# Squares of the residual stream summed by halves, a root chain with one step less, and a wait of GpSimd on its own last piece

## The reference

```python
xf * lax.rsqrt(jnp.mean(xf * xf, axis=-1, keepdims=True) + EPS) * g
```

## Time and profile before

| | us |
|---|---|
| median of three runs (lowest, highest) | 1600.02 (1599.84, 1602.06) |
| the profiled execution | 1606.23 |
| its span, first to last instruction | 1604.4 |
| PE busy (share of the span) | 1527.9 (95%) |
| POOL busy | 1224.2 (76%) |
| ACT busy | 714.9 (45%) |
| DVE busy | 689.3 (43%) |
| mean granted PE clock, as a share of full speed | 0.983 |

### The profile page before, as it was taken

The page is one execution under the profiler, slowest core; times in us unless marked ns, Lnnn a source line. Parts: engine busy times, 40 slices in busy tenths (PEclk is TensorE's granted clock), DMA queues, the critical chain, the costliest instruction groups (busy, mean ns, idle before and its releaser), DMA issues.

```text
span 1604.4 us, 21660 instructions
## 1 busy us (share of the span) xinstructions
PE 1527.9 (95%) x7010; PEld 1165.5 (73%) x7010; DVE 689.3 (43%) x1306; ACT 714.9 (45%) x881; POOL 1224.2 (76%) x1184
## 2 busy tenths in 40 slices
PE   7999999999999999989999999999999899999986
PEld 5777877788887778877788887888785656646535
DVE  3996854311116986834310037265544122122115
ACT  4554453544446544534544455546341422415323
POOL 6998898888899996888888898977591733639623
PEclk9999999999999999999999999998999999999997
DMA  6754454677765553455677655645364998999990
GB/s 210 224 168 135 132 157 134 190 227 214 228 203 162 166 158 117 132 145 152 192 231 217 189 173 172 203 132 171 91 208 152 343 337 341 346 390 396 397 358 28
DMA packets 95958, 333.84 MB, mean 208 GB/s; under 512 B 11184, under 2 KB 15808, under 8 KB 94944
## 3 DMA queue, kind: packets, MB, share of 16 engines
q1 hardware_dynamic: 88240, 307.26, 58.2%
q10 hardware_dynamic: 6480, 21.22, 4.3%
q0 software_dynamic: 1152, 4.19, 0.7%
HBM read 322.12 MB, written 21.00 MB: 214 GB/s over the span
## 4 chain that ended last, share of the span: by engine, by line
POOL 44%; PE 32%; issue 18%; DMA 2%; DVE 2%; ACT 1%; POOLq 1%; ACTq 0%; DVEq 0%; SPq 0%
POOL w_lo L1897 43%; PE bank L691 7%; PE bank L1206 5%; PE bank L695 4%; PE bank L1274 3%; PE bank L1224 3%; PE bank L1243 3%; PE bank L1297 2%; PE bank L1337 1%; DMA arena<-in_experts 1%; DMA logits<-outputs_by_expert,tiny 1%; ACT w_hi L1450 1%; POOL w_lo L1912 1%; PE bank L1106 1%; PE bank L730 1%
## 5 line engine op out<-in xcount | busy, mean ns | idle before, releaser
L1897 POOL TENSOR_TENSOR w_lo<-raw,w_hi 128x256 fp32r<-128x256 f32 (+1 forms) x1092 | 1030.8, 978 | 165.6 <-ACT w_hi L1450 163.1
L1450 ACT ACTIVATE w_hi<-raw 128x1024 fp32r<-128x1024 f32 x371 | 392.8, 1059 | 529.1 <-PE bank L695 283.0
L691 PE MATMUL bank<-w_hi,hT 128*128 128x512 f32 x2240 | 601.4, 401 | 25.4 <-DVE hT L2013 5.9
L691 PEld LDWEIGHTS bank<-w_hi,hT 128*128 128x128 f32 x2240 | 420.8, 192 | 123.0 <-issue 11.8
L695 PE MATMUL bank<-w_lo,hT 128*128 128x512 f32 x1120 | 329.9, 396 | 6.6 <-POOL w_lo L1897 6.5
L695 PEld LDWEIGHTS bank<-w_lo,hT 128*128 128x128 f32 x1120 | 212.5, 191 | 57.5 <-POOL w_lo L1897 12.0
L1912 POOL TENSOR_TENSOR w_lo<-arena,w_hi 128x1024 fp32r<-128x1024 f32 x61 | 144.4, 2388 | 126.5 <-ACT w_hi L1450 126.3
L2316 DVE SCALAR_TENSOR_TENSOR arena<-bank,tiny,arena 128x256 f32<-128x256 f32 x44 | 21.1, 484 | 170.7 <-ACT arena L1611 153.6
L1450 ACT ACTIVATE w_hi<-arena 128x1024 fp32r<-128x1024 f32 x61 | 64.0, 1057 | 57.8 <-PE bank L1206 28.7
L1006 PE MATMUL bank<-w_hi,mixT 128*128 128x512 f32 x352 | 88.0, 390 | 0.0
L691 PE MATMUL bank<-w_hi,mixT 128*128 128x512 f32 x288 | 78.7, 397 | 2.5 <-DVE xn L2290 2.5
(11 more groups left out here) (390 smaller groups left out, 1883.5 us busy)
## 6 DMA issues: line engine op xcount, KB each, us to landing
raw<-in_stream SPq DMA_DIRECT2D x357, 512.0 KB, 3.6
arena<-in_experts SPq DMA_DIRECT2D x154, 512.0 KB, 11.3
raw<-in_experts SPq DMA_DIRECT2D x38, 512.0 KB, 9.5
rows_by_expert<-in_blank ACTq DMA_DIRECT2D x56, 128.0 KB, 3.9
arena<-in_stream SPq DMA_DIRECT2D x9, 512.0 KB, 14.3
gates<-rows_by_expert SPq DMA_DIRECT2D x3, 1024.0 KB, 7.3
outputs_by_expert<-xn ACTq DMA_DIRECT2D x3, 1024.0 KB, 8.4
bias_skewed<-bias_windows SPq DMA_DIRECT2D x4, 512.0 KB, 5.0
```

What stands on the lines that cost most here:

```text
L691: pe.matmul(LIN[t][:, :], lhs[:, a, k0 + k, t * P:(t + 1) * P], w, start=(k0 + k == 0 and a == 0), stop=False)
L1450: act.activation(w_hi[:, s, :], src, ACT.Copy).then_inc(s_hi, 1)
L1897: part = nc.gpsimd.tensor_tensor(w_lo[:, i, c], raw[:, i, c], w_hi[:, i, c].bitcast(F32), ALU.subtract)
```

## The change

- `rounds`: where a quarter is made in more than one piece, GpSimd now waits, after each quarter, until its own last piece has raised s_lo.
- `root_inverse` and `refined`: t = -0.5 t v in one operation, and the result (t + 1.5) r in one. The operation that made -0.5 t + 1.5 by itself is gone. The order of the multiplications is another, the value the same up to rounding.
- `x_stats` calls `both_halves`: the squares of the second half (two of 128 x 512, into columns 2 and 3) and a sum of two columns each. The first half's squares now stand at four places ahead of it: before the first splits of the program; in `x_back`, after the adds of half 0 and a wait on them, ahead of the adds of half 1; and in `layer`, after residual(0), ahead of the second norm's first splits.
- `second` likewise; the subtraction for sw moves behind the first pair of splits, and the squares' scrap output goes to xn in place of xs.

```diff
--- before.py
+++ after.py
@@ -1897,6 +1897,8 @@
                             part = nc.gpsimd.tensor_tensor(w_lo[:, i, c], raw[:, i, c], w_hi[:, i, c].bitcast(F32),
                                                            ALU.subtract)
                         part.then_inc(s_lo, 1)
+                        if parts > 1:
+                            pool.wait_ge(s_lo, r * RING + (i + 1))
 
             per_layer, ff = LAYER_Q // RING, 6 * (FF_GROUPS - 1) // RING
             for l in range(LAYERS):
@@ -1972,10 +1974,13 @@
                 if meanwhile:
                     meanwhile()
                 root_inverse(n)
-                last = dve.tensor_tensor(tiny[:, to:to + n], r, t, ALU.mult)
+                last = refined(tiny[:, to:to + n], r, t)
                 if to == 32:
                     own(last)
                 return last
+
+            def refined(out, r, t):
+                return dve.scalar_tensor_tensor(out, t, 1.5, r, ALU.add, ALU.mult)
 
             def root_inverse(n):
 
@@ -1983,17 +1988,21 @@
                 dve.wait_ge(s_std, std.up())
                 own(dve.reciprocal(r, s))
                 own(dve.tensor_tensor(t, r, r, ALU.mult))
-                own(dve.tensor_tensor(t, t, v, ALU.mult))
-                own(dve.tensor_scalar(t, t, -0.5, 1.5, ALU.mult, ALU.add))
-
-            def x_squares():
+                own(dve.scalar_tensor_tensor(t, t, -0.5, v, ALU.mult, ALU.mult))
+
+            def half_squares(n):
                 for t in range(TT):
-                    i = squares(x[:, t, :], xn[:, t, :], D, t)
+                    cols = slice(n * 512, (n + 1) * 512)
+                    i = squares(x[:, t, cols], xn[:, t, cols], D, 2 * n + t)
                 own(i)
 
+            def both_halves():
+                half_squares(1)
+                own(dve.tensor_tensor(tiny[:, 0:2], tiny[:, 0:2], tiny[:, 2:4], ALU.add))
+
             def x_stats(gain):
 
-                x_squares()
+                both_halves()
                 split(hT, KT // 2, gain, KT // 2)
                 rstd(2, X_INV).then_inc(s_rs, 1)
                 dve.wait_ge(s_rs, rs.up())
@@ -2335,7 +2344,9 @@
                     dve.wait_ge(s_used, pos.up())
                     v = x[:, 1, n * 512:(n + 1) * 512]
                     dve.tensor_tensor(v, AB[2 + n][:, :], v, ALU.add).then_inc(s_x, 1)
-                dve.wait_ge(s_x, xr.up(2))
+                    dve.wait_ge(s_x, xr.up())
+                    if n == 0:
+                        half_squares(0)
 
             def next_gain():
                 dve.wait_ge(s_sm, smc.up(32))
@@ -2491,12 +2503,6 @@
             def rows_normed(t):
                 dve.wait_ge(s_grow, 16)
                 dve.scalar_tensor_tensor(normed_rows[:, t, :], x[:, t, :], tc(X_INV, t), gain_row, ALU.mult, ALU.mult).then_inc(s_norm, 1)
-
-            def half_squares(n):
-                for t in range(TT):
-                    cols = slice(n * 512, (n + 1) * 512)
-                    i = squares(x[:, t, cols], xn[:, t, cols], D, 2 * n + t)
-                own(i)
 
             def place():
 
@@ -2669,11 +2675,10 @@
                 dve.wait_ge(s_x, xr.up(2))
 
             def second():
+                both_halves()
+                split(hT, QK, S_N1, KT // 2)
                 dve.wait_ge(s_sw, 1)
                 dve.tensor_tensor(sw[:, 1, :], small[:, S_SW:S_END], sw[:, 0, :].bitcast(F32), ALU.subtract).then_inc(s_nx, 1)
-                for t in range(TT):
-                    squares(x[:, t, :], xs[:, t, :], D, t)
-                split(hT, QK, S_N1, KT // 2)
                 for t in range(TT):
                     i = dve.tensor_tensor(xn[:, t, :], x[:, t, :], gain1, ALU.mult)
                 own(i)
@@ -2686,8 +2691,8 @@
                 own(dve.tensor_scalar(mean_x, mean_x, EPS, None, ALU.add))
                 dve.scalar_tensor_tensor(mean_xn, mean_x, EPS, mean_xn, ALU.mult, ALU.add).then_inc(s_var, 1)
                 root_inverse(4)
-                dve.tensor_tensor(tiny[:, X_INV:X_INV + 2], tiny[:, 34:36], tiny[:, 50:52], ALU.mult).then_inc(s_rs, 1)
-                own(dve.tensor_tensor(first_inv, tiny[:, 32:34], tiny[:, 48:50], ALU.mult))
+                refined(tiny[:, X_INV:X_INV + 2], tiny[:, 34:36], tiny[:, 50:52]).then_inc(s_rs, 1)
+                own(refined(first_inv, tiny[:, 32:34], tiny[:, 48:50]))
                 dve.wait_ge(s_rs, rs.up())
                 for t in range(TT):
                     dve.tensor_scalar(x[:, t, :], xn[:, t, :], first_inv[:, t:t + 1], None, ALU.mult)
```

## The result

The changed kernel takes **1627.15 us** (median; lowest 1622.64) against 1599.93 (1599.74 to 1602.06) for the kernel before in the same comparison: ratio 1.0153, 95% interval 1.0128 to 1.0178, so 24.5 us slower by the ratio (interval 20 to 28). Forecast was 1602.5, and the range ended at 1608. One execution of the changed kernel took 2829 us at a granted clock of 0.807; the ratio leaves it out, the median of the other three is 1626.96, and nothing here rests on it.

The account below looks back on a forecast made before the run. TensorE was taken as the bound, with GpSimd close behind. Halves in x_back +2.2, root chain -2.8 and GpSimd's wait +3.1 sum to +2.5 on the median of 1600.0: 1602.5 us, range 1596.5 to 1608.

Parts of the forecast that it names:

- GpSimd's wait: At quarter ends in GpSimd's loop: waiting for its own last piece costs +3.1 us, between 0 and 7.0.
- The price: At each quarter's end on GpSimd: 0.12 us lost, from 0.04 of overlap and 0.08 start delay; bounds 0 and 0.20.
- The place: Only GpSimd runs ending in TensorE's wait for w_lo pass the loss on: 26 of 35 quarter ends count.
- 35 quarters in four runs: Four long GpSimd stretches that end in TensorE waiting for w_lo: 140 pieces, 122 us of GpSimd.
- The one cover that I claimed: In those four stretches the vector engine's turns, some 35 of 0.69 us, cover a quarter of the quarter ends.
- GpSimd becomes the bound: Rival, chance 0.30: every quarter end in the four runs costs 0.20 us, nothing covered; +8.1 in all, 1608.1 us.
- The holes feed the vector engine: Rival, chance 0.20: tiny operations in the small norms slip into GpSimd's holes and its price is covered; -4.1, 1595.9 us.
- The halves in x_back: At layer 1's and the second block's start, squaring the first half delays TensorE 1.1 us each: +2.2 us.
- The halves in the hidden places: Before the first splits and the second norm's splits, the squares fall in VectorE's idle time and cost nothing.
- cover of 6.43 us: VectorE's idle time before the split for the second norm, taken to hide the new pair of squares.
- The root chain: One tiny operation fewer in 14 places: 1.4 us at seven norms and tail, 1.4 at small norms; -2.8 us.
- TensorE's clock: After a long gap TensorE may run at 1.2 GHz for a stretch: no shift of the centre, range widened 1.7 us each side.

Follow-up runs that it names:

- e6: The kernel before with GpSimd's wait only after the third quarter of a round, where the loop turns: 1616.11 us, ratio 1.0102.
- e5: The kernel before with GpSimd's wait only after the first and second quarter of a round, not at the loop's turn: 1609.89 us, ratio 1.0056.
- e12: The kernel before with six pieces a quarter in place of four, and GpSimd's wait on the last of each quarter: 1678.73 us, ratio 1.0478.
- e1: The changed kernel without GpSimd's wait, halves and root chain as changed: 1605.2 us, ratio 1.0015 to the kernel before.
- e2: The kernel before with GpSimd's wait alone added: 1629.42 us, ratio 1.0164.
- e4: The kernel before with the squares by halves alone, old root chain and no wait: 1602.72 us, ratio 1.0001.
- e3: The kernel before with the shortened root chain alone: 1601.38 us, ratio 0.9995.
- e9: The changed kernel without GpSimd's wait and with x_back as before, both halves squared in x_stats and second there: 1605.13 us, ratio 1.0030 to the kernel before.
- e10: The kernel before with six quarters in a turn of GpSimd's loop in place of three, no wait: 1605.27 us, ratio 1.0031.
- e7: The kernel before with a wait after every quarter in pieces, but on its third piece of four by a separate semaphore: 1601.1 us, ratio 0.9998.
- e11: The kernel before with six pieces a quarter in place of four, no wait: 1693.12 us, ratio 1.0504.

## Why the prediction was wrong

**GpSimd's wait: the step that failed, in both factors.** Forecast 26 x 0.12 = +3.1 us, upper end 35 x 0.20 = 7.0. Measured alone: +26.

*The price* was 0.12 a quarter from below, 0.20 from above; it is 0.20 inside a turn and up to 0.51 at the turn, 0.30 on average. I had the parts (lost overlap 0.04, a start after a semaphore 0.08), but the steps that run ahead were put only into the upper bound, with 0.08 for all of them. The turn has a compare and a branch more, and e6 shows that turn as the dearer one. The Trainium skill, GPSIMD Engine Reference, section Architecture, had spoken against the change (a completion holds back only what waits on it, and the next instruction is started early); the trace agrees in kind, and by its measure it is more than the overlap that is lost.

*The place* was the larger error. With the true price the forecast's 35 quarters in four runs would still give only 10.5 us. "Elsewhere ScalarE's w_hi waits for TensorE, and the wait hides in GpSimd's idle time" holds in the second block, where the holes cost next to nothing, and not in the layers. ScalarE waited for TensorE in the kernel before for 293.8 us, but for raw for another 196.2, and raw is late because w_lo was. Through that ring a hole outside the four runs comes back too, which is the growth of ScalarE's waits for raw from 196 to 313 us and of TensorE's waits for w_lo from 28 places to 63. I took the places where TensorE waited for w_lo **before** as the only ones where it could wait for it after. e5 and e6 show the share that does come through, about half. The one cover that I claimed holds: where VectorE takes turns (a piece then takes 1.1 us or so), three quarters in a row take 13.7 us from 98.3 us on in the kernel before, and 13.5 with the wait, from 97.9 on.

**The rivals.** "GpSimd becomes the bound" named the side, the engine and both signs (waits for w_lo well over 28, start to start over a quarter's end near 0.90: it is 0.86, and up to 1.17 at the turn), and its 1608.1 missed by 19 us (16 by the ratio) for the two reasons above. "The holes feed the vector engine" is true as a mechanism and was given too little thought: I argued from the tiny operations of a chain, and wrote of those that wait that they have their turn today. They need not have it, and they gain (9.66 to 0.69 us, 101 us of busy time in e12). In a kernel with four pieces that is worth a few us at most: e1 to after is 1.0138 by the ratios, e2 1.0164, a difference of 4 us that the intervals don't separate.

**The halves in x_back, +2.2.** Right in mechanism. 0.8 us late in the profile after, gaps of 0.72 to 0.92 us at both places in three kernels: 0.7 to 0.9 each in place of 1.1. The time of e4, +0.2 us (-2.6 to +3.0), can't tell this from nothing. The pair took 2.2 us in place of 2.3, and what follows it starts before the one ahead has ended.

**The halves in the hidden places, 0.** The reason failed: "2 x 1.21 us at most" came from one pair that had its turns, and the same pair can take 10.9 us, which no cover of 6.43 us hides (TensorE's gaps of 2.29 and 1.59 us in e4). In the changed kernel the wait prevents it, so the 0 holds there (1.0 us mean for the 28 squares).

**The root chain, -2.8.** The chains did shorten and the gaps behind them by 0.4 to 0.9 us, about 1.9 in all in e3. The time shows -0.8 (interval -3.2 to +1.6). Root and halves together, forecast -0.6, gave +2.4 (0 to +4.8) in e1; without the halves in x_back, forecast -2.8, it was +4.8 (+2.6 to +6.9) in e9.

**TensorE's clock** played no part in the loss: 0.983 before, 0.988 after. The 1.7 us for one stretch at the lower level was too much. The first six products behind the gap of 2.28 us took 2.90 us at a granted 0.50; in e3, behind a gap of 1.37, the clock stayed at 1.00 and they took 1.63. So the stretch cost about 1.3 us.

**Open.** When VectorE gets a turn between GpSimd's pieces and when it has none: both kinds stand in the same traces, a few us apart (9.65 and then 1.21). That starved operations are what makes e1, e9 and e10 slower than their parts add up to is argued from single traces, each of which has such an operation, and not tested by itself. For it speaks that TensorE idles 72.8, 67.9 and 69.5 us in these three traces against 65.5 before; against it, that e3 and e4 have such operations too and are level with the kernel before. Why the second block lets hardly a hole through is argued from GpSimd's smaller load there, and not tested. No version beat the kernel before; the root chain alone is level with it.

## What to carry to other kernels

A wait of an engine on its own last instruction costs the time of whatever it does ahead, not that of a wait: price it with the loop's branch included, or wait on the instruction before the last (e7), which cost nothing measurable. In a ring, never count only the places where the consumer waits today: a hole in the producer also delays the next load. Here half of the time of all holes came through: nearly all of that in the layers, where GpSimd was busy for 86 to 90% of the time, and next to nothing in the second block, where it was busy for 81%. And where one engine's operations can be held up by another's, look for the longest instance of a cheap operation, not its mean: one 0.69 us operation at 9.65 us tells more than the group's average.

## What was unexpected of the hardware

- An operation of VectorE can wait behind a long run of GpSimd's subtractions: 13 pieces and 9.65 us, 21 pieces and 11.65, 35 pieces and 18.0 us for a scan on 4 partitions at 591.5 us of e11. The first got in when GpSimd paused for 0.37 us. With pieces of 170 columns twelve operations lasted over 3 us, with pieces of 256 three.
- GpSimd's end-to-start over a loop's turn is 0.36 to 0.47 us with the wait and hidden without it; inside the turn it is 0.16 us.
